# Row scales and transposes of x token block by token block, and more of the first adaLN row blocks summed on TensorE

## The reference

```python
def rmsnorm(x, g):
    xf = x.astype(jnp.float32)
    y = xf * lax.rsqrt(jnp.mean(xf * xf, axis=-1, keepdims=True) + EPS)
    return (y * g.astype(jnp.float32)).astype(x.dtype)
...
mod = jax.nn.silu(c) @ w_ada[l] + b_ada[l]
sh1, sc1, ga1, sh2, sc2, ga2 = jnp.split(mod[:, None, :], 6, axis=-1)
h = rmsnorm(x, ln_mix_g[l]) * (1.0 + sc1) + sh1
... = jnp.split(h @ w_in[l], IN_SPLITS, axis=-1)
```

## Time and profile before

| what | value |
|---|---|
| median of 3 runs | 696.66 us (695.89 to 696.75) |
| the profiled execution | 696.22 us, its span in the trace 694.4 us |
| TensorE busy | 681.8 us, 98% of the span |
| weight loads (PEld) busy | 570.5 us, 82% |
| VectorE busy | 331.3 us, 48% |
| ScalarE busy | 225.9 us, 33% |
| HBM read | 85.41 MB |

### The profile page before, as it was taken

How to read it: one execution, slowest core, us unless ns; L and a number is a source line. 1 busy time by engine, 2 the same in 40 slices (tenths; PEclk the granted TensorE clock), 3 DMA queues, 4 the chain that set the end, 5 groups by cost and what they waited for, 6 DMA issues and landing times.

```text
span 694.4 us, 9147 instructions
## 1 busy us (share of the span) xinstructions
PE 681.8 (98%) x3653; PEld 570.5 (82%) x3653; DVE 331.3 (48%) x572; ACT 225.9 (33%) x384; POOL 187.4 (27%) x95
## 2 busy tenths in 40 slices
PE   8999999999999999999999999999999999999996
PEld 7889889887787888888988888888888888888885
DVE  4798888755587773626212531101000049533126
ACT  3637332240333433326422322222222122332224
POOL 2000000000000001050254445444444338455521
PEclk9999999999999999999999999999999999999999
DMA  9988978520000001760054545433432213331003
GB/s 307 354 320 292 365 265 290 193 95 32 1 1 1 2 1 57 245 184 1 22 160 125 165 136 151 122 91 92 125 118 92 91 61 122 100 111 63 1 1 121
DMA packets 74539, 88.10 MB, mean 127 GB/s; under 512 B 3113, under 2 KB 57601, under 8 KB 74369
## 3 DMA queue, kind: packets, MB, share of 16 engines
q1 hardware_dynamic: 73184, 85.31, 37.8%
q0 software_dynamic: 416, 1.08, 0.5%
q10 hardware_dynamic: 896, 1.12, 0.4%
HBM read 85.41 MB, written 2.10 MB: 126 GB/s over the span
## 4 chain that ended last, share of the span: by engine, by line
PE 94%; DVE 3%; ACT 1%; issue 1%; DMA 0%; POOLq 0%; POOL 0%; SPq 0%; DVEq 0%; ACTq 0%
PE ps L1255 13%; PE ps L1257 13%; PE ps L1256 13%; PE ps L1687 12%; PE ps L1688 12%; PE ps L1689 12%; PE ps L1426 5%; PE ps L1266 1%; PE ps L1483 1%; PE ps L1375 1%; PE ps L1560 1%; PE ps L1401 1%; PE ps L1469 1%; PE ps L1277 1%; DVE acc L778 1%
## 5 line engine op out<-in xcount | busy, mean ns | idle before, releaser
L441 POOL TENSOR_TENSOR wl<-raw,wh 128x1024 fp32r<-128x1024 f32 x66 | 172.3, 2614 | 203.5 <-ACT wh L490 203.4
L1687 PE MATMUL ps<-hTh,wh 128*128 128x512 f32 (+1 forms) x384 | 143.6, 374 | 0.0
L1689 PE MATMUL ps<-hTh,wl 128*128 128x512 f32 (+1 forms) x384 | 142.6, 371 | 0.0
L1688 PE MATMUL ps<-hTl,wh 128*128 128x512 f32 (+1 forms) x384 | 142.6, 371 | 0.0
L490 ACT ACTIVATE wh<-raw 128x1024 fp32r<-128x1024 f32 x94 | 97.0, 1040 | 105.0 <-PE ps L1689 74.0
L1185 DVE TENSOR_TENSOR act<-ps,sg 128x512 f32<-128x512 f32 x22 | 15.2, 691 | 195.1 <-PE ps L1689 195.1
L1255 PE MATMUL ps<-wh,hTh 128*128 128x512 f32 (+2 forms) x232 | 89.4, 385 | 1.2 <-DVE hTl L832 1.1
L1257 PE MATMUL ps<-wh,hTl 128*128 128x512 f32 (+2 forms) x232 | 86.4, 372 | 0.0
L1256 PE MATMUL ps<-wl,hTh 128*128 128x512 f32 (+2 forms) x232 | 86.3, 372 | 0.0
L1687 PEld LDWEIGHTS ps<-hTh,wh 128*128 128x128 f32 x384 | 72.3, 188 | 12.9 <-issue 0.5
L1688 PEld LDWEIGHTS ps<-hTl,wh 128*128 128x128 f32 x384 | 72.3, 188 | 12.7 <-issue 0.5
(11 more groups left out here) (198 smaller groups left out, 888.3 us busy)
## 6 DMA issues: line engine op xcount, KB each, us to landing
raw<-in_w_ada SPq DMA_DIRECT2D x32, 512.0 KB, 5.3
raw<-in_w_ff_gate SPq DMA_DIRECT2D x22, 512.0 KB, 3.9
raw<-in_w_ff_up SPq DMA_DIRECT2D x22, 512.0 KB, 3.8
raw<-in_w_ff_down SPq DMA_DIRECT2D x22, 512.0 KB, 3.2
raw<-in_w_in SPq DMA_DIRECT2D x20, 512.0 KB, 7.9
early<-in_w_ada SPq DMA_DIRECT2D x16, 512.0 KB, 9.4
raw<-in_w_out SPq DMA_DIRECT2D x8, 512.0 KB, 4.1
xs<-in_x SPq DMA_DIRECT2D x4, 512.0 KB, 5.5
```

The lines of the kernel that those rows point to most:

```text
L441: pool.tensor_tensor(lo, raw[:, slot, 0:n], hi.bitcast(F32), ALU.subtract).then_inc(w_lo2, 1)
L1687: mm(o, hi[:, ks], hTh[:, k, c0:c1], start=k == 0, stop=False)
L1688: mm(o, hi[:, ks], hTl[:, k, c0:c1], start=False, stop=False)
L1689: ins = mm(o, lo[:, ks], hTh[:, k, c0:c1], start=False, stop=k == KT - 1)
```

## The change

Four things are changed in the head of the kernel, all in front of the ninth unit of the input projection.

1. The scales of x are made block by block: four variances, four powers of 128x1 on GpSimd, and each diag[t] as soon as its scale is there (block 1 on VectorE, the others on ScalarE). TensorE transposes six feature blocks (`X_FIRST`) of token block 0, then three warm matmuls, six of block 1, the transpose of the small vectors (`rows`), six of block 2 and of block 3, then k = 4; k = 7 comes behind `modulation(0)`. Before, it took all 32 after the last scale, by feature block. `WARM` goes from (9, 8) to (9, 3).
2. `ADA_ON_PE` becomes a list: four of the eight row blocks of quarter 0 and two of those of quarter 1 are multiplied on TensorE.
3. VectorE reads the sums (`quarter(q)`) earlier in its order: that of quarter 0 directly behind its own row blocks, that of the others between `low(2q)` and `low(2q + 1)`.
4. ScalarE rounds unit 1 (`high(1)`) after the second feature block and not before the first.

```diff
-ADA_ON_PE = 2
-WARM = (9, 8)
+ADA_ON_PE = [4, 2, 0, 0]
+ADA_DONE = [sum(KT - n for n in ADA_ON_PE[:q]) for q in range(UPC + 1)]
+WARM = (9, 3)
+X_FIRST = [0, 1, 2, 3, 5, 6]
+X_ORDER = X_FIRST + [4, 7]
...
-            power(N_X, rstd[:, :])
+            for t in range(TT):
+                power(N_X + t, rstd[:, t:t + 1])
...
-            ada_early(0, range(KT - ADA_ON_PE))
-            ada_early(1, range(2))
+            ada_early(0, range(KT - ADA_ON_PE[0]))
             quarter(0)
             low(0)
             h_low(0)
-            ada_early(1, range(2, 3))
+            ada_early(1, range(2))
             h_low(1)
             low(1)
-            ada_early(1, range(3, KT))
+            ada_early(1, range(2, KT - ADA_ON_PE[1]))
             for q in range(1, UPC):
 
                 low(2 * q)
+                quarter(q)
                 low(2 * q + 1)
-                quarter(q)
...
             def modulation(q):
 
-                pe.wait_ge(ada_used, KT * (q + 1) - ADA_ON_PE)
                 if q:
                     pe.wait_ge(mod_read, q)
-                sum_columns(0, 4 * q, (2 * q, 2 * q + 1), q == 0)
-                sum_columns(1, 4 * q + 2, (2 * q, 2 * q + 1), q == 0).then_inc(mod_sum, 1)
+                for i in range(2 if ADA_ON_PE[q] else 0):
+                    first_columns(q, i)
+                pe.wait_ge(ada_used, ADA_DONE[q + 1])
+                joined = ADA_ON_PE[q] > 0
+                sum_columns(0, 4 * q, (2 * q, 2 * q + 1), joined)
+                sum_columns(1, 4 * q + 2, (2 * q, 2 * q + 1), joined).then_inc(mod_sum, 1)
+
+            def first_columns(q, i):
+
+                j = 4 * q + 2 + i
+                pe.wait_ge(early_in[j % EARLY], 16 * (j // EARLY + 1))
+                for n in range(2):
+                    for kk in range(4 - ADA_ON_PE[q], 4):
+                        c = 4 * q + 2 * i + n
+                        c0 = (2 * kk + n) * P
+                        mm(ps[:, 7, c:c + 1], early[:, j % EARLY, c0:c0 + P], cs[:, 4 + kk:5 + kk],
+                           start=i == 0 and n == 0 and kk == 4 - ADA_ON_PE[q], stop=False)
...
+            for t in range(TT):
+                if t == 1:
+                    warm(WARM[1])
+                if t == 2:
+                    pe.wait_ge(rows_in, 16 * 2)
+                    pe.wait_ge(biases_in, 16 * 4)
+                    pe.transpose(ps[:, 4, 0:P], rows[:, :], ident).then_inc(rowsT, 1)
+                if t == 1:
+                    pe.wait_ge(xn_done, 1)
+                else:
+                    pe.wait_ge(xn_done2, (t + 3) // 2)
+                for k in X_FIRST:
                     x_transpose(k, t)
-
-            x_transposes(0)
-            pe.wait_ge(c_silu, 1)
-            first_columns(0)
-            first_columns(1)
+            pe.wait_ge(cols_ok, 1)
+            for t in range(TT):
+                x_transpose(X_ORDER[KT - 2], t)
             modulation(0)
-            x_transposes(3)
-            pe.wait_ge(cols_ok, 1)
-            for k in range(4, KT):
-                x_transposes(k)
+            for t in range(TT):
+                x_transpose(X_ORDER[KT - 1], t)
```

More of the change, by code:

```diff
@@ L165, in block_kernel @@
         junk = at("junk", [P, D], F32, R + 74)
-        diag = at("diag", [P, TT, P], F32, R + 74)
+        diag = at("diag", [P, TT, P], F32, R + 48)
         QTh = at("QTh", [P, HPG, T], F32R, R)
@@ L500, in _, with x_diag, x_squares @@
             a.activation(cs[:, :], ps[:, 5, 0:KT], ACT.Silu).then_inc(c_silu, 1)
-            for t in range(0, TT, 2):
+            def x_diag(t):
+                a.wait_ge(rstd_ok, N_X + t)
+                a.activation(diag[:, t, :], ident, ACT.Copy, scale=rstd[:, t:t + 1]).then_inc(xn_done2, 1)
+            def x_squares(t):
                 a.wait_ge(x_in[t], 16)
@@ L505, in _ @@
                 a.activation(junk[:, :], xs[:, t, :], ACT.Square, accum_out=ssq[:, t:t + 1]).then_inc(sq_done, 1)
+            x_squares(0)
             a.wait_ge(ident_in, 16)
             a.activation(identR[:, :], ident, ACT.Copy).then_inc(consts_r, 1)
-            a.wait_ge(rstd_ok, N_X)
-            for t in (2, 3):
-                a.activation(diag[:, t, :], ident, ACT.Copy, scale=rstd[:, t:t + 1]).then_inc(xn_done2, 1)
+            x_diag(0)
+            x_squares(2)
+            x_diag(2)
+            x_diag(3)
             def x_copy(k):
-                a.wait_ge(xT_ps, k + 1)
+                a.wait_ge(xT_ps, X_ORDER.index(k) + 1)
                 a.activation(xT[:, k, :], ps[:, x_bank(k), :], ACT.Copy).then_inc(xT_ok, 1)
-            for k in range(4):
+            for k in X_ORDER[0:KT - 1]:
                 x_copy(k)
             high(0)
-            high(1)
             for k in range(KT):
                 a.wait_ge(mod_read, k // 2 + 1)
-                a.wait_ge(xT_ok, k + 1)
+                a.wait_ge(xT_ok, X_ORDER.index(k) + 1)
                 if k >= 2:
@@ L529, in _ @@
                 if k == 1:
-                    for n in range(4, KT):
-                        x_copy(n)
+                    high(1)
+                    x_copy(X_ORDER[KT - 1])
                 if k % 2 and k < KT - 1:
@@ L804, in mod_columns, with x_squares @@
                 return d.tensor_tensor(dst, dst, cols[:, g_off + k0:g_off + k1], ALU.mult)
-            for t in range(1, TT, 2):
+            def x_squares(t):
                 d.wait_ge(x_in[t], 16)
@@ L809, in _, with x_variance @@
                                             scalar=0.0, op0=ALU.mult, op1=ALU.add, accum_out=ssq[:, t:t + 1]))
-            d.wait_ge(sq_done, TT // 2)
-            d.tensor_scalar(rstd[:, :], ssq[:, :], 1.0 / D, EPS, ALU.mult, ALU.add).then_inc(var_ok, 1)
+            def x_variance(t):
+                if t % 2 == 0:
+                    d.wait_ge(sq_done, t // 2 + 1)
+                d.tensor_scalar(rstd[:, t:t + 1], ssq[:, t:t + 1], 1.0 / D, EPS, ALU.mult, ALU.add).then_inc(var_ok, 1)
+            x_variance(0)
+            x_squares(1)
+            x_variance(1)
+            d.wait_ge(rstd_ok, N_X + 1)
+            d.tensor_scalar(diag[:, 1, :], ident, rstd[:, 1:2], None, ALU.mult).then_inc(xn_done, 1)
+            x_variance(2)
+            x_squares(3)
+            x_variance(3)
             d.wait_ge(rowsT, 1)
@@ L817, in _ @@
                 then(d.tensor_scalar(cols[:, off:off + KT], cols[:, off:off + KT], 1.0, None, ALU.add))
-            d.wait_ge(rstd_ok, N_X)
-            for t in range(TT // 2):
-                d.tensor_scalar(diag[:, t, :], ident, rstd[:, t:t + 1], None, ALU.mult).then_inc(xn_done, 1)
             def mod_rows(n, ga, half, bank=7):
@@ L1265, in warm @@
                 for _ in range(n):
[L1266 to L1273, removed]
+                    mm(ps[:, 7, 0:2 * P], ones[:, :], BD[:, 0, :], start=True, stop=True)
             def sum_columns(i, c0, ks, joined=False):
@@ L1298, in x_transpose @@
                     ins.then_inc(xT_ps, 1)
-            def x_transposes(k):
-                for t in range(TT):
-                    x_transpose(k, t)
[L1305 to L1314, removed]
-            x_transposes(0)
-            pe.wait_ge(c_silu, 1)
-            first_columns(0)
-            first_columns(1)
+            pe.wait_ge(ones_set, 3)
+            warm(WARM[0])
+            pe.wait_ge(c_silu, 1)
+            for t in range(TT):
[10 more added lines that the diff above has]
+                for k in X_FIRST:
+                    x_transpose(k, t)
+            pe.wait_ge(cols_ok, 1)
+            for t in range(TT):
+                x_transpose(X_ORDER[KT - 2], t)
             modulation(0)
-            x_transposes(3)
-            pe.wait_ge(cols_ok, 1)
-            for k in range(4, KT):
-                x_transposes(k)
+            for t in range(TT):
+                x_transpose(X_ORDER[KT - 1], t)
             def sum_rows(g, half, bank=7):
```

17 lines of the change are left out of this document (8 added, 9 removed).

## The result

The changed kernel takes 701.67 us (median of 6, 701.01 to 702.47), the kernel before 696.31 (median of 6, 695.89 to 696.75): ratio 1.0077, 95% interval 1.0067 to 1.0087. It is 5.4 us slower. The profiled execution took 701.90 us, with a span of 700.1 us against 694.4.

What follows compares the result with a forecast made beforehand. TensorE was taken as the bound, 94% of the chain, with head delays passed on to the end. Profiled 696.22 plus 2.6 gave 698.8, 699.3 against the median; the forecast was 699.0 us, own range 697.8 to 700.4, wider range 695.9 to 701.6.

Steps and rivals of the forecast that it cites:

- the rival that the clock falls: TensorE from 17.75 us: one-column matmuls, then gaps, drop it to 1.2 GHz, costing 2.9 us; time 701.9, chance 0.14.
- a sum at full clock: Whole head of the kernel: added work and gaps delay the end by 2.6 us, with no clock fall; chance 0.51.
- The prediction's own sign of it: Products between 25 and 32 us standing 0.4 apart instead of 0.23 would show the forecast wrong.
- the gaps and the mixed one-column matmuls of before: Argument against a clock fall: earlier TensorE gaps of 0.96 and 0.78 us and mixed one-column matmuls brought none.
- second triple: In each quarter's first unit; forecast starts 27.0, 38.9 and 49.15 us, that is 1.15, 2.45 and 2.55 late.
- the sum at 21.02: Sum of quarter 0 on TensorE, forecast to start at 21.33 instead of 18.15 us and be read at 22.4.
- the gaps at 2.11 and 1.29 us: TensorE idle ahead of the first and second triple of quarter 0, forecast as 2.1 and 1.2 us.
- Cheaper one-column matmuls: Rival: in a long row they cost half, 0.056 us a load; 695.7, no measurable change; chance 0.23 with smaller errors.
- VectorE sets the pace and gains: Rival: VectorE's four fewer row operations in the head save 3.4 us; time 692.8, chance 0.12.
- The 81 ns of the Trainium skill: Price per load and matmul pair: 48 one-column pairs would cost 3.9 instead of 5.4 us, loss near 1.1.
- a loss of 2.3 us: Kernel before: VectorE reads quarter 0's sum, started at 18.15, only at 21.59; about 2.3 us lost, mostly hidden by TensorE.
- The order on VectorE: Quarters 1 to 3: low(3) moved behind mods costs nothing where VectorE waits for the sum, but shortens its slack behind it.

Runs made afterwards that it cites:

- e10: Changed kernel with one-column matmuls of quarters 0 and 1 made 128 wide, plus six warm matmuls in the two gaps behind quarter 0's sum: 698.52 us, ratio 1.0030.
- e7: Kernel before, with four instead of two row blocks of quarter 0 on TensorE: four executions, 697.87, 701.00, 700.61 and 700.53 us.
- e9: Changed kernel with 24 row-block matmuls and 8 sum matmuls of quarters 0 and 1 made 128 columns wide: 698.80 us, ratio 1.0042.
- e2: Changed kernel with row blocks on TensorE in quarter 0 alone, [4, 0, 0, 0]: 698.36 us, ratio 1.0026.
- e8: e6 with the sums of quarters 1 to 3 read behind low(2q + 1) again, as before the change: 696.66 us.
- e6: Changed kernel with only two row blocks on TensorE, [2, 0, 0, 0], and six warm matmuls filling two gaps: 696.59 us, ratio 1.0001.
- e4: Changed kernel with the sums of quarters 1 to 3 read behind low(2q + 1) again: 700.32 us, ratio 1.0064.
- e12: e6 with its eight one-column matmuls placed between transposes, singly but for one pair: 696.23 us, ratio 1.0001.
- e1: Changed kernel with its one-column matmuls mixed among transposes (quarter 0) and products of unit 0 (quarter 1): 700.11 us, ratio 1.0055.

## Why the prediction was wrong

**The step that failed is the weighing of the rival that the clock falls**, with 0.14, so that the forecast stood on a sum at full clock, in which falls cost nothing. The runs show 3.2 us for them. The prediction's own sign of it came true: the products at 27 to 30 us stand 0.43 apart and not 0.23. What I put against it was that the gaps and the mixed one-column matmuls of before brought no fall. But the earlier trace rows show at most eight loads of one-column matmuls in a row, with transposes right behind them, and the change makes 40, at 16.81 and 20.45, with little behind. The rows bore out nothing for such a stretch. The Trainium skill (TensorE: Matmul & The Clock Gate, Part 1: The HAM clock gate) lets the clock fall back when the engine has not been busy. Here it fell at 20.3 while TensorE had been without a gap since 9.16. The rival's time, 701.9, was the measured one within 0.3 us, but in part by luck: it had one fall of 2.9 us, priced by the start of the kernel and brought on by gaps; in the profiled execution there were two, 10.2 and 3.4 us long, the first of them ahead of the gaps, and together with a start 0.2 us later they put the second triple of quarter 1 at 42.15, 3.3 us behind that of e10.

**What the fall cost, from e10.** From the second triple of quarter 0 to the row blocks of quarter 1 the changed kernel takes 33.32 - 27.01 = 6.31 us, e10 4.68: 1.6 us. From the sum of quarter 1 (35.22) to the second triple it takes 6.93, e10 5.48 (33.39 to 38.87): 1.45 us, the second fall. The rest, 0.2 us, is the later start. Sum 3.3 of the 5.7 us. By medians all falls together cost 701.67 - 698.52 = 3.2 us, and e7 has 2.8 between executions of one program. The rows of e10 in the timeline:

```profile
21.02 0.97 PEld L1298 LDWEIGHTS ps<-ones,acc 128*128 128x128 f32 x8
...
22.22 0.16 DVE L816 TENSOR_TENSOR mods<-ps,cols 128x2 f32<-128x2 f32 x1 [4.18 <-PE ps L1298]
...
31.49 1.98 PEld L1321 LDWEIGHTS ps<-cs,early 128*128 128x128 f32 x16
33.39 0.97 PEld L1298 LDWEIGHTS ps<-ones,acc 128*128 128x128 f32 x8
```

**The sum at full clock was right.** I had the second triples at 27.0, 38.9 and 49.15; e10 has them at 26.81, 38.87 and 49.08, and its time is 2.2 us over the kernel before, its span 2.6, where I had 2.6. The steps hold one by one: e10 has the sum at 21.02 (forecast 21.33), its reading at 22.22 (22.4), and 4.28 us from the reading in quarter 1 (34.59) to the second triple (4.4); e9 has the gaps at 2.11 and 1.29 us (2.1 and 1.2). The unit of quarter 0 takes 4.63 us by the rows and not 4.65, which changes nothing. In the changed kernel the second triple at 27.01, as forecast, is luck: the sum started at 20.45 and not at 21.33, since TensorE was sooner at full pace in that execution (the ninth warm matmul ended by 8.7 and not by 10.0, and TensorE even waited 0.48 us for diag[0]), and the fall took 0.8 us of this back, with the eight loads of the sum in 1.71 us instead of 0.89. That first rise is read from the pace of the warm loads alone: the windows give a granted clock of 1.00 for the first 10 us too.

**The other rivals.** Cheaper one-column matmuls: no, 0.112 in a row of 32 (e2, 17.01 to 20.59). VectorE sets the pace and gains: no, e2 gives back two of its operations and is faster. The 81 ns of the Trainium skill (TensorE: Matmul & The Clock Gate, Back-to-back issue gap): the runs go by 0.112 for a load and matmul of these float32 products.

**A reading that was wrong without hurting the sum.** I called VectorE's reading at 21.59 a loss of 2.3 us. ScalarE's copy and two high() held hf until 22.24 anyway, 0.2 us behind mods (ready at 22.0), and e7 shows the same. In the timeline of the kernel before, behind the copy at 20.24:

```profile
20.74 1.61 ACT L490 ACTIVATE wh<-raw 128x1024 fp32r<-128x1024 f32 x2
```

The change took away a wait that was covered, and paid for it on the engine that is the bound.

**The order on VectorE** for quarters 1 to 3 is worth nothing with two row blocks on TensorE (e8 against e6). In the changed kernel itself that is not shown: e4 took 1.4 us less by the median, and its traces explain the gain by the clock only for one pair of executions.

What stays open: why the clock falls in some executions of one program and not in others (e9, e12, and e7 by its mean clocks). The traces show when it fell and what TensorE did before; no run settles how much of which work would keep it up.

## What to carry to other kernels

Moving small work to the engine that is the bound costs it in full, and what it frees elsewhere is worth only what was waited for there. A one-column matmul cost TensorE as much time here as a transpose of 128 columns (0.112 us a load) and, in a long row or ahead of a gap, its clock as well. Making it wide cost no time that shows and kept the clock up longer (e9), filling the gaps did the rest (e10); mixing alone did not (e1). Read the granted clock by windows of a few microseconds, since a mean of 0.99 over the span hid 3 us here. When a rival rests on a stretch that the trace doesn't have, its absence from the trace is no evidence against it.

## What was not expected of the hardware

The clock fell at 20.3 us while TensorE was without a gap, behind a row of one-column matmuls 0.112 us from load to load, and making the same matmuls 128 columns wide, at the same distance, took that fall away (e9, 2.9 us). It stayed at 1.2 GHz for about 10 us in the changed kernel, though products without a gap ran from 27 us on, and for 3.4 us in e6, where warm matmuls filled the gap. One program gave 697.87 us at a mean clock of 0.999 and 700.5 to 701.0 us at 0.991 to 0.993 (e7).
